# Expert weights streamed through a ring on one core: w_down's halves read as 16 KB rows in place of 8 KB rows

## What is computed

```python
def moe(h, w_router, b_router, w_gate, b_gate, w_up, b_up, w_down, b_down):
    ...
    gate = jnp.einsum('td,edf->tef', t, w_gate) + b_gate
    up = jnp.einsum('td,edf->tef', t, w_up) + b_up
    gate = jnp.minimum(gate, SWIGLU_LIMIT)
    up = jnp.clip(up, -SWIGLU_LIMIT, SWIGLU_LIMIT)
    act = (up + 1.0) * gate * jax.nn.sigmoid(SWIGLU_ALPHA * gate) * comb[..., None]
    out = jnp.einsum('tef,efd->td', act, w_down) + comb @ b_down
```

## Time and profile before

| | |
|---|---|
| time, median of 3 runs (lowest, highest) | 1128.36 us (1128.35, 1129.87) |
| span of the profiled execution, first to last instruction | 1127.6 us |
| busy: TensorE matmuls, VectorE, ScalarE | 83%, 30%, 21% of the span |
| mean granted TensorE clock | 0.935 |
| HBM read, written | 448.27 MB, 2.18 MB |
| DMA packets, in all | 41936, 451.56 MB |
| chain that ended last, by engine | PE 48%, DMA 33%, DVE 12%, SP's queue 3% |

### The profile page before, as it was taken

How to read it: one execution, slowest core, us unless ns; L and a number is a source line. 1 busy time by engine, 2 the same in 40 slices (tenths; PEclk the granted TensorE clock), 3 DMA queues, 4 the chain that set the end, 5 groups by cost and what they waited for, 6 DMA issues and landing times.

```text
span 1127.6 us, 32284 instructions
## 1 busy us (share of the span) xinstructions
PE 932.5 (83%) x13926; PEld 557.6 (49%) x13927; DVE 339.3 (30%) x819; ACT 240.3 (21%) x401; POOL 28.3 (3%) x29
## 2 busy tenths in 40 slices
PE   3899698799997878997878779999956999686873
PEld 1577574455553534553544445555523555353531
DVE  7899833322221111221212112222211222111213
ACT  4364722211111111111111101111100111110111
POOL 2001012000000000000000000000000000000000
PEclk8899799799998989999898989999988999998986
DMA  9738999899999999999999999999999999999996
GB/s 377 317 150 335 341 345 394 353 425 425 427 426 424 426 427 427 425 427 427 427 429 426 424 426 427 426 427 425 425 427 426 427 427 425 424 427 426 425 427 197
DMA packets 41936, 451.56 MB, mean 400 GB/s; under 512 B 4426, under 2 KB 4938, under 8 KB 6362
## 3 DMA queue, kind: packets, MB, share of 16 engines
q1 hardware_dynamic: 41162, 450.28, 96.1%
q10 hardware_dynamic: 432, 0.57, 0.2%
q0 software_dynamic: 320, 0.39, 0.2%
HBM read 448.27 MB, written 2.18 MB: 399 GB/s over the span
## 4 chain that ended last, share of the span: by engine, by line
PE 48%; DMA 33%; DVE 12%; SPq 3%; issue 2%; ACT 1%; DVEq 0%; ACTq 0%
DMA ring<-in_w_down 33%; PE ps L946 20%; PE ps L977 13%; PE ps L601 3%; PE ps L878 3%; SPq L515 3%; PE ps L825 2%; PE ps L678 2%; DVE scan_w L1384 2%; PE ps L812 1%; DVE upc L1537 1%; DVE acts L1541 1%; DVE upc L1534 1%; DVE actT L1545 1%; DVE scan_p L1386 1%
## 5 line engine op out<-in xcount | busy, mean ns | idle before, releaser
L946 PE MATMUL ps<-ring,XT 128*32 128x256 f32 x6528 | 404.1, 400 | 73.0 <-DMA ring<-in_w_gate 38.0
L946 PEld LDWEIGHTS ps<-ring,XT 128*32 128x32 f32 x6528 | 217.4, 115 | 226.3 <-DMA ring<-in_w_gate 44.5
L977 PE MATMUL ps<-ring,actT 128*32 128x256 f32 x3264 | 198.5, 395 | 30.5 <-DMA ring<-in_w_down 27.7
L977 PEld LDWEIGHTS ps<-ring,actT 128*32 128x32 f32 x3264 | 102.9, 113 | 110.6 <-DMA ring<-in_w_down 30.7
L1532 DVE TENSOR_SCALAR gcl<-ps 128x256 f32<-128x256 f32 x51 | 21.7, 425 | 274.7 <-PE ps L946 274.7
L1534 DVE TENSOR_SCALAR upc<-ps 128x256 f32<-128x256 f32 x51 | 21.7, 425 | 256.3 <-PE ps L946 256.3
L1217 ACT COPY selT<-ps 128x256 f32<-128x256 f32 x51 | 19.0, 372 | 337.0 <-PE ps L601 337.0
L1214 ACT ACTIVATE sgm<-gcl 128x256 f32<-128x256 f32 x51 | 21.3, 417 | 211.2 <-DVE gcl L1532 211.2
L1214 ACT ACT_TABLE_LOAD x51 | 65.4, 1283 | 3.1 <-DVEq L1495 2.3
L1219 ACT COPY ys<-ps 128x256 f32<-128x256 f32 x51 | 19.0, 373 | 211.4 <-PE ps L977 211.4
L922 PE MATMUL ps<-ys,selT 32*128 32x256 f32 x832 | 62.2, 415 | 0.5 <-ACT ys L1219 0.5
(11 more groups left out here) (250 smaller groups left out, 709.6 us busy)
## 6 DMA issues: line engine op xcount, KB each, us to landing
ring<-in_w_gate SPq DMA_DIRECT2D x64, 2048.0 KB, 29.3
ring<-in_w_up SPq DMA_DIRECT2D x64, 2048.0 KB, 34.8
ring<-in_w_down SPq DMA_DIRECT2D x64, 2048.0 KB, 38.5
ring<-in_w_ada SPq DMA_DIRECT2D x11, 2048.0 KB, 9.8
wout<-in_w_out SPq DMA_DIRECT2D x1, 4096.0 KB, 20.3
w<-in_w_in SPq DMA_DIRECT2D x2, 1536.0 KB, 21.3
wglu<-in_w_glu SPq DMA_DIRECT2D x1, 2304.0 KB, 13.6
spare<-in_w_ada SPq DMA_DIRECT2D x1, 2048.0 KB, 24.5
```

The costliest lines, as they stand in the source:

```text
L946: ins = pe.matmul(out[32 * fq:32 * fq + 32, :], XT[:, k % 2, (k // 2) * 32:(k // 2) * 32 + 32], w(i)[:, k % 4, fq * QU:(fq + 1) * QU], sta ...
L977: ins = pe.matmul(pY[32 * dq:32 * dq + 32, :], actT[:, k % 2, (k // 2) * 32:(k // 2) * 32 + 32], w(i)[:, k % 4, dq * QU:(dq + 1) * QU], st ...
```

## The change

The host orders the rows of every `w_down` matrix so that the four rows of a partition follow one another (quarter and partition are exchanged within a half). The kernel then reads a half of down with the same pattern as one of gate or up: 128 rows of 16 KB in place of 128 x 2 rows of 8 KB. The bytes, the units, their order, the slots, what lies in each slot and all matmuls are as before. Line numbers below the change are smaller by up to 12.

```diff
@@ laid_out
     biases = np.concatenate([x['b_gate'][0], x['b_up'][0], x['b_down'][0]], axis=1)
+    down = x['w_down'].reshape(1, NE, 2, 2, P, 2, D).transpose(0, 1, 2, 4, 3, 5, 6).reshape(1, NE, D, D)
...
-            ("b_router", x['b_router']), ("w_gate", x['w_gate']), ("w_up", x['w_up']), ("w_down", x['w_down']),
+            ("b_router", x['b_router']), ("w_gate", x['w_gate']), ("w_up", x['w_up']), ("w_down", down),
@@ build
         def slot(turn, i):
 
-            r = ring[HOME[turn][i]][:, :, :]
-            if i < 4:
-                return r.rearrange("p k c -> p (k c)")
-            return r.rearrange("p (q k) c -> p q (k c)", q=2)
+            return ring[HOME[turn][i]][:, :, :].rearrange("p k c -> p (k c)")
 
         def half_of(w, i):
 
-            if i < 4:
-                return w.rearrange("(b p k) c -> b p (k c)", b=2, p=P)[i % 2]
-            return w.rearrange("(b q p k) c -> b p q (k c)", b=2, q=2, p=P)[i % 2]
+            return w.rearrange("(b p k) c -> b p (k c)", b=2, p=P)[i % 2]
@@ sync, the loop over experts
                     for i in range(UNITS_E):
                         w = W6[i][0][0]
-                        if i < 4:
-                            src = w.rearrange("e (b p k) c -> e b p (k c)", b=2, p=P)[bass.ds(e, 1), i % 2]\
-                                .rearrange("e p x -> (e p) x")
-                        else:
-                            src = w.rearrange("e (b q p k) c -> e b p q (k c)", b=2, q=2, p=P)[bass.ds(e, 1), i % 2]\
-                                .rearrange("e p q x -> (e p) q x")
+                        src = w.rearrange("e (b p k) c -> e b p (k c)", b=2, p=P)[bass.ds(e, 1), i % 2]\
+                            .rearrange("e p x -> (e p) x")
                         sp.wait_ge(unit_used[i], done)
                         sp.dma_start(slot(turn, i), src).then_inc(unit_in[turn][i], 16)
```

## The result

| | kernel before | changed kernel |
|---|---|---|
| median of 5 runs (lowest, highest), us | 1129.33 (1128.35, 1130.3) | 1125.06 (1124.09, 1126.51) |
| ratio, 95% interval | | 0.9966 (0.9954 to 0.9979) |
| span of the profiled execution, us | 1127.6 | 1123.0 |

The change makes the kernel 0.34% faster, and the interval of the ratio excludes 1. Two later sets of runs of the same kernel, each beside the kernel before on its chip, gave 0.9951 (0.9935 to 0.9967) and 0.9951 (0.9940 to 0.9963).

What follows compares the result with a forecast made beforehand. The prediction took the never-idle DMA engines as the bound: 62 down units saving 0.075 us each, 4.65 us, with other terms at nothing, bring the span to 1123.0 and the time to 1123.8 us, range 1122.0 to 1126.0.

Steps and rivals of the forecast that it cites:

- The bound: Loop over experts: DMA engines never pause, share 1.01 at 426 GB/s, so the end moves only with the units' pitches.
- The pitch: Down units in the unbroken stretch: 4.970 us each falls to gate and up's 4.895, 0.075 us less.
- The count: Units in the unbroken stretch: 60 of the loop and two of expert 1, 62 x 0.075 = 4.65 us saved.
- The loss at the last unit: Last two down units, tail's loads right behind: 1.76 us lost, left as it is in the sum.
- rival 4: Last two down units: their loss changes by itself, by -1.76 to +1.76 us, giving 1122.0 to 1125.6 us; 10%.
- the tail after the last landing: End of the kernel, 1108.96 to 1127.6 us: claimed not to be touched by the change.
- Nothing given back: DMA queue in the loop: the unit ahead lands 7.1 and 8.4 us after an issue, so saving 4.65 us makes none late.
- Rival 3: Stretch at 700 to 800 us: TensorE's clock falls; two rounds at 1.2 GHz give 7.5 us more, 1135.9 us; 3%.
- Rival 2: Down units: whole transfer size decides, row length does nothing; time stays at 1128.4 us; 3%.
- rival 1: Down units: half or less of the 0.075 us is row length, slots and place stay; 1126 to 1127 us; 7%.
- the carrying over from span to median: Whole kernel: the runs' median was taken as 0.8 us above the span, turning 1123.0 into 1123.8 us.
- the estimate of 3.5 ns: Down's packets: some 3 cycles each at 850 MHz, 0.028 us a unit, 1.7 us in all, or 1126.6 us; not used.

Runs made afterwards that it cites:

- tail_wait: Changed kernel with the tail's loads (gate, residual and gain rows) issued only after the last down unit has landed; ratio to the kernel before 0.9948, median 1123.09 us.
- gate_8k: Changed kernel with gate read in two pieces of 8 KB, 1 MB apart, down keeping 16 KB rows; ratio to the kernel before 0.9997, median 1128.85 us.
- down_8k_near: Changed kernel with down read in two 8 KB pieces again, laid 12 KB apart start to start; ratio to the kernel before 0.9996, median 1128.21 us.
- all_8k: Changed kernel with gate, up and down all read in two pieces of 8 KB, 1 MB apart; ratio to the kernel before 1.0078, median 1137.41 us.

## Why the prediction was right

- **The bound.** The stream of weights is not interrupted, and the end moves with its pitch: confirmed by rows of 4, 8 and 16 KB, whose pitches and loops follow the number of packets, and by a DMA share of 1.01 in each of them (1.00 with rows of 32 KB).
- **The pitch.** Down's pitch was to fall from 4.970 to 4.895 us; two units take 9.79 us, as foretold, and the sum of six 29.37 us.
- **The count.** 62 units by 0.075 us gave 4.65 us. The profiled spans differ by 4.6 us, but that agreement is partly luck: 0.63 us of it is the first part, which ended earlier (206.77 in place of 207.40). The rest shrank by 4.0 us. The loop, with 60 of the 62 units, gave 4.7 us (4.5 by the count). Two terms at the end were missed. The loss at the last unit, which the prediction left at 1.76 us with a bound of +1.76 (rival 4), is now 12.02 - 9.79 = 2.23 us, 0.47 more; tail_wait showed that the loads behind it cause it, not why it grew. And the tail after the last landing, "that the change does not touch", grew from 18.64 to 19.08 us, 0.44 more, by 16 matmuls that took 2.09 us in place of 1.64; that they ran slower in all three profiles of the changed kernel (1.96 to 2.09 us) is seen, and why the clock came back later for them is not shown.
- **Nothing given back.** The shortest time from issue to landing after 335 us is 14.4 us (13.3 before), and in 210 to 335 us it is 11.1 us (12.0 before), still more than twice the 4.9 us of a unit; the DMA share is 1.01, so the engines did not run dry. Rival 3 did not come: the stretch without waits kept its clock of 1.00. The prediction put its threshold at about one and a half rounds; by its own numbers it is (8.4 + 4.65) / 10.3 = 1.3.
- **Rivals 1 and 2.** Rival 2 fell with the change itself, which moved down's pitch, and rival 1 with gate_8k. The rival that the prediction did not have, the jump of 1 MB, fell with down_8k_near. The difference follows the number of packets.
- **The size in the median.** The measured drop is 1129.33 - 1125.06 = 4.3 us (5.4 and 5.1 in the two later sets), but the time is 1125.06 and not 1123.8: inside the range of 1122.0 to 1126.0, and 0.3 us above the 1123.2 to 1124.8 that the prediction gave its own forecast. The step that was off is the carrying over from span to median: it took 0.8 us between them. In each run of the changed kernel the time lies 1.8 to 1.9 us above that run's own span (1124.81 and 1123.0 in the profiled one); the three runs of before that were known then happened to include the lowest of five, and their median has since moved up by 1.0 us.
- **Beside the Trainium skill.** 8 KB beside 16 KB rows cost 9.3 ns a packet here, and 4 KB rows 9.2 ns. The Trainium skill (DMA: Bandwidth & Descriptors, Why small descriptors are slow) states some 3 cycles a packet; the estimate of 3.5 ns from it is too small for the whole cost of a packet in this case. Taking 8 packets at 9.3 ns off the 4.895 us of a unit leaves 2.097 MB in 4.82 us, 435 GB/s, an estimate from these rows. The Trainium skill (DMA: Bandwidth & Descriptors, Where 436 GB/s comes from) states a ceiling of 435 GB/s, and the estimate agrees with it.

## What to carry to other kernels

When the DMA engines are full from end to end, a unit's pitch can be read off the waits of the engine that consumes it, and the difference between two forms of the same size, times their number, is the gain in the stream; what follows its last transfer can add or take half a us to a whole one, as it did here. Rows can still be too short at 8 KB: each packet cost about 9.3 ns here, 1.5% at 8 KB beside 16 KB, so let the host lay weights out such that a partition's share of a transfer is one run, and try merging neighbouring units where their consumer has slack, with an eye on the first merged transfer, which is issued later. Compare kernels from the point at which the bound begins: the scatter of what comes before it can be as large as the gain.

## What was not expected of the hardware

- The cost of a packet is the same within what can be read for rows of 4, 8 and 16 KB, and rows of 32 KB fit it: 2 MB took 5.115, 4.97, 4.895 and 4.855 us, with 32, 16, 8 and 4 packets of data an engine (at 32 KB the number of DMAs was halved too).
- SP's queue took transfers further ahead where they had fewer packets. The longest issue to landing in 335 to 1067 us was 34.9 us with all rows of 8 KB, 39.2 with down in rows of 4 KB (as many packets in all), 43.6 in the kernel before and 51.0 in the changed kernel. With gate and up in rows of 32 KB it was 56.3 us, and no issue there took longer than 0.35 us, so in that run the queue was not what held SP back. What sets the limit was not tried.
- The tail's loads (four of 128 KB into 32 partitions each, one of 1 MB, one of 512 KB), queued right behind the last unit, made that unit land late although they were issued after it: by 1.8 us in the kernel before and by 2.2, 2.4 and 2.1 us in the three profiles of the changed kernel. Which of the three kinds of load does it was not tried.
- The tail after the last landing took between 17.7 and 19.1 us in the ten profiles whose tail loads are issued as before, and all of the difference is two groups of matmuls that ran at one or the other clock. The last 32 of down and the 16 of the scatter took 3.64 + 2.09 us in the changed kernel (tail 19.08 us) and 3.27 + 1.15 us in all_8k (17.85 us); the tail less these two groups is 13.3 to 13.4 us in all ten.
